# Where the modulation rows stand between the steps of a fused two-block kernel: no row in an attention step, and some rows sooner

## The reference

```
mod  = silu(c) @ w_ada + b_ada            # one vector of 3 x 2048: shift, scale, gate
h    = norm(x) * (1 + scale) + shift
proj = h @ w_in                           # 256 x 2048 times 2048 x 4096..8192
y    = attention(proj) * silu(z)
x    = x + gate * (y @ w_out)             # then a norm
```

## Time and profile before

| | us |
|---|---|
| median of three executions | 1512.79 |
| the profiled execution, its own time | 1513.1 |
| its span, first to last instruction | 1511.3 |
| TensorE busy | 1429.5 |
| VectorE busy | 1180.6 |
| ScalarE busy | 708.7 |

### The profile page before, as it was taken

The page is one execution under the profiler, slowest core; times in us unless marked ns, Lnnn a source line. Parts: engine busy times, 40 slices in busy tenths (PEclk is TensorE's granted clock), DMA queues, the critical chain, the costliest instruction groups (busy, mean ns, idle before and its releaser), DMA issues.

```text
span 1511.3 us, 19093 instructions
## 1 busy us (share of the span) xinstructions
PE 1429.5 (95%) x6634; PEld 1181.9 (78%) x6634; DVE 1180.6 (78%) x1472; ACT 708.7 (47%) x990; POOL 115.7 (8%) x215
## 2 busy tenths in 40 slices
PE   4899999999998899999999999889999999999996
PEld 3677878877887688888888888778788888888885
DVE  5998799587999988788666758898788865557566
ACT  4464454554433444444556643344344544455431
POOL 1111001002000001000010100000000000000000
PEclk9999999999999899999999999989999999999998
DMA  9999989788999499999766678849899786555762
GB/s 388 414 413 412 344 338 374 245 298 294 392 394 376 175 374 358 381 378 359 268 210 207 208 274 311 326 176 371 315 352 358 236 292 209 180 182 153 259 193 92
DMA packets 99869, 448.84 MB, mean 297 GB/s; under 512 B 11424, under 2 KB 13776, under 8 KB 76496
## 3 DMA queue, kind: packets, MB, share of 16 engines
q1 hardware_dynamic: 69840, 249.33, 46.2%
q0 software_dynamic: 26352, 185.63, 31.6%
q10 hardware_dynamic: 3600, 12.85, 2.1%
HBM read 445.65 MB, written 2.12 MB: 296 GB/s over the span
## 4 chain that ended last, share of the span: by engine, by line
PE 81%; DVE 10%; issue 3%; DMA 2%; ACT 2%; POOL 0%; DVEq 0%; ACTq 0%
PE bank L716 22%; PE bank L718 22%; PE bank L717 21%; DVE gw L1297 4%; PE bank L678 3%; PE bank L680 2%; PE bank L679 2%; PE bank L889 2%; PE bank L837 2%; DVE w_lo L1289 1%; DMA raw<-in_t_steps 1%; PE bank L692 1%; DVE w_lo L1282 1%; PE bank L846 1%; DVE area L1297 1%
## 5 line engine op out<-in xcount | busy, mean ns | idle before, releaser
L962 ACT CAST w_hi<-raw 128x1024 fp32r<-128x1024 f32 x464 | 485.9, 1051 | 690.1 <-PE bank L718 582.9
L1282 DVE TENSOR_TENSOR w_lo<-raw,w_hi 128x1024 fp32r<-128x1024 f32 x380 | 461.0, 1222 | 271.6 <-ACT w_hi L962 270.7
L716 PE MATMUL bank<-w_hi,act_hi 128*128 128x512 f32 x1536 | 614.8, 400 | 4.6 <-DVE w_lo L1282 3.6
L718 PE MATMUL bank<-w_hi,act_lo 128*128 128x512 f32 x1536 | 600.7, 391 | 0.0
L717 PE MATMUL bank<-w_lo,act_hi 128*128 128x512 f32 x1536 | 599.1, 390 | 0.0
L1297 DVE CUSTOM_DVE_ANT_0 gw<-gw,c_act 128x2048 f32<-128x2048 f32 x170 | 388.1, 2284 | 3.5 <-DMA gw<-in_t_ada 3.5
L716 PEld LDWEIGHTS bank<-w_hi,act_hi 128*128 128x128 f32 x1536 | 289.3, 188 | 63.8 <-DVE w_lo L1282 3.7
L718 PEld LDWEIGHTS bank<-w_hi,act_lo 128*128 128x128 f32 x1536 | 288.8, 188 | 62.1
L717 PEld LDWEIGHTS bank<-w_lo,act_hi 128*128 128x128 f32 x1536 | 289.4, 188 | 57.9
L1289 DVE TENSOR_TENSOR w_lo<-raw,w_hi 128x1024 fp32r<-128x1024 f32 x84 | 101.8, 1219 | 20.9 <-ACT w_hi L962 20.7
L678 PE MATMUL bank<-w_hi,act_hi 128*128 128x512 f32 x256 | 101.6, 397 | 5.8 <-DVE w_lo L1289 5.8
(11 more groups left out here) (151 smaller groups left out, 952.7 us busy)
## 6 DMA issues: line engine op xcount, KB each, us to landing
raw<-in_t_steps SPq DMA_DIRECT2D x464, 512.0 KB, 5.4
gw<-in_t_mod POOLq DMA_DIRECT2D x96, 1024.0 KB, 7.8
gw<-in_t_ada POOLq DMA_DIRECT2D x42, 1024.0 KB, 8.1
gw<-in_t_kv_mod POOLq DMA_DIRECT2D x32, 1024.0 KB, 6.6
area<-in_t_ada POOLq DMA_DIRECT2D x6, 1024.0 KB, 12.8
area<-gate_rows ACTq DMA_DIRECT2D x3, 1024.0 KB, 12.8
area<-in_ln_g ACTq DMA_DIRECT2D x2, 1024.0 KB, 6.7
area<-in_ln_b ACTq DMA_DIRECT2D x2, 1024.0 KB, 9.7
```

The source lines that it names most:

```text
L716: nc.tensor.matmul(dst, hi, w_hi[:, j % LEAD, k], start=(kt == 0), stop=False)
L718: return nc.tensor.matmul(dst, lo, w_hi[:, j % LEAD, k], start=False, stop=(kt == KT - 1))
L962: nc.scalar.copy(w_hi[:, b], raw[:, j % SLOTS]).then_inc(hi_ready, 1)
L1282: nc.vector.tensor_tensor(w_lo[:, j % SLOTS], raw[:, j % SLOTS], w_hi[:, j % LEAD].bitcast(F32), ALU.subtract).then_inc(lo_ready, 1)
```

## The change

Two things. gemv_steps lists the half steps between the first and the last one that hold no step of an attention, and spreads a pair's rows over that list alone; where there are more rows than such half steps, two rows fall into one. And PAIR_TILES has other numbers: in sum still 144.

```diff
-PAIR_TILES = {2: 2, 3: 7, 4: 7, 5: 9, 6: 9, 7: 7, 8: 7, 9: 7, 10: 7, 11: 7, 12: 7, 13: 7, 14: 3, 15: 3, 16: 3, 17: 4,
-              18: 5, 19: 7, 20: 8, 21: 8, 22: 4, 23: 5, 24: 4, 25: 4, 26: 3}
+PAIR_TILES = {2: 2, 3: 7, 4: 7, 5: 8, 6: 10, 7: 8, 8: 6, 9: 8, 10: 8, 11: 8, 12: 8, 13: 8, 14: 4, 15: 4, 16: 3, 17: 5,
+              18: 3, 19: 6, 20: 4, 21: 8, 22: 3, 23: 5, 24: 4, 25: 4, 26: 3}
...
     begin, end = {2: (10, 16), 4: (1, 12), 5: (4, 16), 22: (0, 7)}.get(pair, (1, 14))
-    return [(begin + i * ((end - begin) / n), first + i) for i in range(n)]
+
+    halves = [h for h in range(begin, end) if not in_attention(pair, h)]
+    return [(halves[i * len(halves) // n], first + i) for i in range(n)]
+
+
+def in_attention(pair, h):
+    return any(h + PAIR_STEPS * (pair - p) in at for p, at in zip(ATTENTION_PAIR, STEP_AT))
```

## The result

| | before | after |
|---|---|---|
| median, 11 executions each, us | 1512.87 (1510.44 to 1516.51) | 1517.31 (1516.60 to 1521.92) |
| ratio, 95% interval | | 1.0034 (1.0025 to 1.0043) |
| the profiled execution, its own time, us | 1513.1 | 1521.92 |
| its span, us | 1511.3 | 1520.1 |

The forecast was 1514.1 (1508 to 1519): the side is right, the size 3.2 us short. Of the three outcomes that the prediction gives chances to, it is the slower one (above its line of 0.2%, 3.0 us), which had 0.30; "same" had 0.48.

What follows compares the result with a forecast made beforehand. TensorE, busy 95% of the span, was taken to bound the kernel, so only its stops and lower clock count. Terms -5.7 - 1.3 + 2.2 + 1.6 + 2.7 + 1.8 = +1.3 us put 1512.8 at 1514.1, range 1508 to 1519.

Steps and rivals of the forecast that it cites:

- rival (b): Pairs 6 and 7: DMA of added rows makes weights land late and stops TensorE; +4.5 on the forecast, 1518.6; chance 0.20.
- Pair 20, -5.7: Pair 20, 8 rows to 4: TensorE's wait for a late w_lo and the clock drop behind it go; -5.7 us.
- Pair 6, first half, -1.3: Pair 6, first half: TensorE's waits for VectorE's retention copies shrink as GpSimd's root comes sooner; -1.3 us.
- Pair 5, +2.2 and +1.6: Pair 5: scores come 2.21 us later, gap grows to 4.6 us, +2.2; lower clock for 3.4 us behind it, +1.6.
- Pairs 14 and 15, +2.7: Pairs 14 and 15: rows ahead of probability copies delay transposes, three times 0.6, and 0.9 at (15,8); +2.7 us.
- Pair 6 to 7, VectorE late, +1.8: Pair 6, second half: two more rows on busy VectorE make the w_lo for (7,1) late for TensorE; +1.8 us.
- Pairs 9 to 13 at no cost: Pairs 9 to 13 with 8 rows: VectorE needs 35.9 us of 43.5, so the rows cost 0.
- rival (c): Pairs 9 to 13 become bound by DMA, five times +1.9 us, 1523.5; chance 0.04.
- Rival (d): Pair 20: the norm rows alone keep it late, so the change doesn't help there; 1519.8; chance 0.04.
- (a): Faster: row shifts in pairs 14, 15 and 7 are hidden, clock stays up in pair 5; -4.8, 1508.0; chance 0.22.
- if pair 7 loses over 4 us: Pair 7: one of the prediction's signs that it is wrong, a loss there of over 4 us.

Runs made afterwards that it cites:

- e4: Kernel before with only pair 20 cut from eight rows to four, the four moved to pairs 10 to 13; 1508.35 us against 1512.87 for before.
- e9: Changed kernel's placing rule with the kernel before's numbers of rows per pair; 1516.58 us against 1512.81 for before.
- e1: Changed kernel with pair 5's eight rows in half steps 4, 5, 6, 9, 11, 11, 13, 15; 1513.69 us against 1512.59 for before.
- e5: Changed kernel with the edits of e1, e2 and e3 together; 1510.93 us against 1512.87 for before.
- e10: e5 with the loads of rows 49 to 79 fetching the next row's data from memory; 1509.74 us against 1512.94 for before.
- e11: e7 with the loads of rows 49 to 79 fetching the previous row's data from memory; 1507.56 us against 1512.94 for before.
- e7: e5 with one row moved sooner, pair 5 having nine rows and pair 6 eight; 1506.41 us against 1512.87 for before.
- e3: Changed kernel with the four rows of pairs 14 and 15 in half steps 1, 5, 9, 13; 1515.56 us against 1512.59 for before.
- e6: Changed kernel with loads of the 18 rows of pairs 6 and 7 bringing only half of each row; 1513.76 us against 1512.87 for before.
- e2: Changed kernel with one row from pair 6 and one from pair 7 moved to pair 8, rows re-placed there; 1516.03 us against 1512.59.
- e8: e7 with pair 5's row of half step 6, directly ahead of the scores, moved behind the attention step; 1504.53 us against 1512.81 for before.
- e0: Changed kernel run again without edit; 1517.78 us against 1512.59 for before.

## Why the prediction was right and where it was short

The result lies within the stated range, but 0.3 us above the narrower one (1510.5 to 1517) that had the chance of 0.50, and nearer to rival (b)'s 1518.6 than to the forecast. Item by item:

**Pair 20, -5.7: right.** -6.0 in the profiles, with no gap and the clock at 1.00; alone -4.5 (e4). With eight rows under the new rule the gap is there (e9), so it was the number of rows.

**Pair 6, first half, -1.3: right.** The gap of 0.42 is gone, 1.59 became 0.61, which stays as I said. The cause is the one named: VectorE's copies no longer wait for GpSimd's root (0.62 and 0.88 us in before, together 1.5). The second of them, in before at 362.93 with its wait, is in after:
```profile
366.08 0.87 DVE L1628 TENSOR_SCALAR area<-bank,rstd 128x256 f32<-128x256 f32 x2
```
The pair gained 1.6 (e9); in after 0.9, since (6,15) already has 0.7 of the next item.

**Pair 5, +2.2 and +1.6: right.** The gap is 4.54 (forecast 4.6) and the lower clock came, for 6.8 us instead of the 3.4 that I took; the pair lost 4.9, for 3.8. The base was worth less than its one profile shows: the gap of 2.3 us is followed by half clock in e1, e4, e5, e10 and e11 (67.5 us) and not in before and e7 (65.9). In e1 the pair got 3.4 us shorter, with the drop still there; the 4.1 of its medians has 2.0 of pair 7 in it and can't price this item alone.

**Pairs 14 and 15, +2.7: right.** 0.53, 0.54 and 0.80 for my three of 0.6, and at (15,8) from 0.47 to 1.32, for 0.9. Sum 3.2 in the profile, 2.2 in the medians (e3).

**Pair 6 to 7, VectorE late, +1.8: right.** 2.0 (e6).

**Pairs 9 to 13 at no cost: right for 11 to 13.** These are 43.52 us long in every profile, pair 11 of e4 at 399 GB/s and a share of 0.99; rival (c) is out. Pair 10 is 0.5 to 1.0 us longer in four of the twelve profiles with eight rows there (after, e2, e3, e8), with a wait of 0.5 to 0.6 at (10,15) in three of them, and in neither of the two with seven (before, e9); whether the eighth row costs this is open. Rival (d) and, by all of the above, (a) are out too.

**Pair 4, nothing: 0.4 missing.** The sum has no term for it, though its rows move too. In every profile with the new rule (4,10) is 0.4 us longer, with a wait of TensorE for probs_t of 0.2 to 0.3; in before and e4 there is none.

**What failed: rival (b) stood beside the sum where it belonged in it.** I gave it 0.20 as another way for things to go, and priced it at +4.5. It came on top: 4.0 to 4.9 in pair 7 in the profiles, 3.5 to 4.3 in the medians (e6), and this is what the forecast was short by (3.2 us). In the pairs that the change touches (4 to 7, 14, 15, 20) the second profile of after is 7.1 us longer than that of before. That the medians are only 4.4 to 5.2 apart fits before's pair 5, which is 1.6 us longer wherever the clock drops. The prediction's own line "if pair 7 loses over 4 us" was met. The profile of before had it: in pair 7 the DMA share was already 1.02, and ScalarE waited for weights four times. That is a reason to put the bytes into the sum; it is no price yet, as e9 shows with one row more there for 0.2 us.

**What stays open.** Why the same number of rows costs so differently. Counted are the rows of pairs 5 and 6 up to (6,6), and those from there to the end of pair 7: 14 and 11 in before, 13 and 11 in e7 and e8 (no loss); 12 and 14 in after, e1 and e3 (3.4 to 6.2 us, 1.3 of it VectorE's); 12 and 12 in e2 and e5 (3.7 and 3.8); 13 and 12 in e9 (0.2). So more rows ahead and fewer behind is the direction, but twelve behind cost 0.2 or 3.8. The source addresses carry 0.8 of it (e10). The rest may lie in when each load is issued. For it: e1, which moves rows of pair 5 only, takes 2.0 us off pair 7. And, counted from (6,4), the loads of e9 corresponding to e5's at 32.6, 36.5 and 40.7 us go at 30.8, 35.0 and 38.9. This was only read, not tried by itself.

## What to carry to other kernels

Work that is moved off a busy engine brings its transfers along. Where the engine that uses them already waits for data, put the bytes into the sum itself and not only into a rival. As a price they are rough: at 2.5 us a row three rows more are 7.6 us where 4.0 to 4.9 were lost, and one row more is 2.5 where 0.2 to 3.8 were. A DMA share near 1.0 over a whole pair does not tell either: pair 11 of e4 (0.99) and pair 7 of e7 (1.01) lost nothing. The time at which each load is issued seems to matter as much as the number (not tried by itself).

The best placing (e8, -8.3 us with the same 144 rows) has a row in half step 4 of pair 5, where VectorE idles, and none ahead of the scores. And behind a gap that is to go, look for the second in line on every engine of the chain before taking the whole of it.

## What the runs showed of the hardware

The same loads of 1 MB and 512 KB, issued at the same moments from neighbouring places in memory, took 6.4 or 8.9 us and 4.6 or 9.4 us from issue to landing (e10, e5), while the core moved 355 and 354 GB/s in those 13.5 us. The other way round (e7, e11) it was 6.8 and 8.5 us, and 5.6 and 8.3, at 361 and 352 GB/s. These are medians of three and five loads. The Trainium skill (DMA: Bandwidth & Descriptors, "Latency and other measured facts") tells of a row pitch in memory at large powers of two that halves the rate of a copy. Here the sources are whole blocks and the rate fell by 0 to 3%, while single loads took up to twice as long; whether two streams meet in the same part of memory no run here shows.

TensorE's clock fell to its lower level, 1.2 of 2.4 GHz, behind pair 5's gap of 2.3 us in five profiles of seven with that gap (for 3.4 us), and behind the one of 4.54 us in all of six with it, then for twice as long. How long it lasts does not follow from the gap alone: behind pair 20's it was 6.8 us after 2.92 (before) and 3.4 after 2.95 (e9). In pair 7 it fell behind gaps of 1.84, 2.29 and 2.30 us (e0, after, e3) and not behind 1.70 and 1.72 (e10, e1). A median over executions therefore has part of the cost of a short gap in it that a single profile can miss.
